# Second residual block: the gated unit's result and the new residual are transposed chunk by chunk, and the FFN norm's inverse root is applied after the up projection

## What is computed

```python
def second_block(x, ...):
    ...
    attn_out = attn @ w_attn_proj
    y = gelu(s5_scan(u, ...))
    ssm_out = (y @ w_glu_val) * sigmoid(y @ w_glu_gate)            # the gated unit
    mixed = sigmoid(g[:, :, 0]) * attn_out + sigmoid(g[:, :, 1]) * ssm_out
    h = h + mixed @ w_out                                          # the second residual
    m = h * rsqrt(mean(h * h, -1) + 1e-6) * norm_ffn               # the FFN norm
    h = h + (silu(m @ w_ffn_gate) * (m @ w_ffn_up)) @ w_ffn_down
    return h * rsqrt(mean(h * h, -1) + 1e-6) * norm_final
```

## Time and profile before

| | |
|---|---|
| median of 3 runs | 3183.25 us (3182.97 to 3200.63) |
| the profiled execution: its own time | 3179.22 us |
| the profiled execution: its span | 3177.4 us |
| TensorE busy (matmuls) | 3016.8 us, 95% of the span |
| VectorE, ScalarE, GpSimd busy | 57%, 40%, 10% |
| share of TensorE in the chain that ended last | 89% |
| mean granted TensorE clock | 0.97 of full speed |

### The profile page before, as it was taken

One profiled execution on the slowest core, in us unless ns is written; L12 is line 12 of the kernel. 1 busy time (PEld: TensorE's weight loads), 2 busy tenths in 40 slices (PEclk: granted clock), 3 DMA queues, 4 the chain that ended last, 5 costly groups with the idle time before them and its releaser, 6 DMA issues.

```text
span 3177.4 us, 43194 instructions
## 1 busy us (share of the span) xinstructions
PE 3016.8 (95%) x18045; PEld 2606.3 (82%) x18045; DVE 1804.6 (57%) x1704; ACT 1272.2 (40%) x1155; POOL 321.1 (10%) x460
## 2 busy tenths in 40 slices
PE   8899999996999999999698999989998999999998
PEld 3588777875999999888587888867877999999886
DVE  1376777787677776544545446754544444444444
ACT  0134544433444444344333333434433444444433
POOL 1000000001000000000105816620000000000000
PEclk9999999997999999999798999999998999999999
DMA  9777777893666655655345652226643555555564
GB/s 356 277 281 260 286 284 274 305 386 137 249 242 225 236 199 187 226 211 201 133 170 180 220 184 77 84 73 217 244 160 132 197 188 197 191 192 211 201 213 168
DMA packets 110499, 671.55 MB, mean 211 GB/s; under 512 B 23521, under 2 KB 25697, under 8 KB 33313
## 3 DMA queue, kind: packets, MB, share of 16 engines
q1 hardware_dynamic: 101584, 626.96, 54.7%
q0 software_dynamic: 8800, 42.97, 3.6%
HBM read 652.48 MB, written 17.40 MB: 211 GB/s over the span
## 4 chain that ended last, share of the span: by engine, by line
PE 89%; DVE 5%; DMA 3%; ACT 1%; issue 1%; SPq 0%; POOL 0%; DVEq 0%; POOLq 0%; ACTq 0%
PE acc L1800 27%; PE acc L1801 26%; PE acc L1802 26%; PE ms L1870 3%; PE tp L1845 2%; DVE w_lo L1130 1%; DMA w_raw<-ada_stream 1%; DMA w_raw<-w_stream 1%; DVE mod_sum L1205 1%; PE ms L2235 1%; PE acc L2264 0%; PE acc L2274 0%; DVE y L1171 0%; DMA ada<-ada_stream 0%; PE ms L2234 0%
## 5 line engine op out<-in xcount | busy, mean ns | idle before, releaser
L1130 DVE TENSOR_TENSOR w_lo<-w_raw,w_hi 128x2048 fp32r<-128x2048 f32 x484 | 1111.6, 2304 | 850.3 <-ACT w_hi L755 831.4
L755 ACT ACTIVATE w_hi<-w_raw 128x2048 fp32r<-128x2048 f32 x484 | 923.5, 1915 | 1071.3 <-DMA w_raw<-w_stream 1069.6
L1800 PE MATMUL acc<-h2T_hi,w_lo 128*128 128x256 f32 x2816 | 785.0, 279 | 3.5 <-DVE h2T_lo L1144 3.5
L1801 PE MATMUL acc<-h2T_lo,w_hi 128*128 128x256 f32 x2816 | 784.5, 279 | 0.0
L1802 PE MATMUL acc<-h2T_hi,w_hi 128*128 128x256 f32 x2816 | 784.4, 279 | 0.0
L1800 PEld LDWEIGHTS acc<-h2T_hi,w_lo 128*128 128x128 f32 x2816 | 530.3, 188 | 4.0 <-issue 4.0
L1801 PEld LDWEIGHTS acc<-h2T_lo,w_hi 128*128 128x128 f32 x2816 | 532.5, 189 | 0.0
L1802 PEld LDWEIGHTS acc<-h2T_hi,w_hi 128*128 128x128 f32 x2816 | 531.9, 189 | 0.0
L1800 PE MATMUL acc<-w_hi,hid_lo 128*128 128x512 f32 x704 | 275.1, 391 | 4.5 <-DVE w_lo L1130 4.5
L1801 PE MATMUL acc<-w_lo,hid_hi 128*128 128x512 f32 x704 | 274.8, 390 | 0.0
L1802 PE MATMUL acc<-w_hi,hid_hi 128*128 128x512 f32 x704 | 274.7, 390 | 0.0
(11 more groups left out here) (503 smaller groups left out, 3968.9 us busy)
## 6 DMA issues: line engine op xcount, KB each, us to landing
w_raw<-w_stream SPq DMA_DIRECT2D x484, 1024.0 KB, 4.8
ada<-ada_stream SPq DMA_DIRECT2D x64, 1024.0 KB, 6.9
w_raw<-ada_stream SPq DMA_DIRECT2D x32, 1024.0 KB, 4.8
g_dram<-gates_out SPq DMA_DIRECT2D x12, 512.0 KB, 7.0
gates_in<-g_dram POOLq DMA_DIRECT2D x12, 512.0 KB, 5.9
bias_rows<-b_in POOLq DMA_DIRECT2D x18, 256.0 KB, 6.2
x_res<-x POOLq DMA_DIRECT2D x2, 2048.0 KB, 13.6
g_dram<-gate_stage SPq DMA_DIRECT2D x8, 512.0 KB, 6.0
```

The costliest lines, as they stand in the source:

```text
L755: sc.activation(whi[:, s % 4], raw[:, s % 4], ACT.Copy).then_inc(hi_made, 1)
L1130: v.tensor_tensor(wlo[:, s % 4], raw[:, s % 4], whi[:, s % 4].bitcast(F32), ALU.subtract).then_inc(lo_made, 1)
L1800: mm(o, sl, mh, start=start, stop=False, skip_group_check=share)
L1801: mm(o, sh, ml, start=False, stop=False, skip_group_check=share)
```

## The change

- The transposes of `mix2` are issued in quarters (two rounds, one chunk's worth): quarters 0 to 2 between the gate and the value chunk of the next pair, quarter 3 after the second group of the first out2 chunk. The copies out of PSUM go with them on ScalarE and VectorE.
- The raw residual `x` is transposed in the same way: quarter n-1 after the second group of out2 chunk n, the last quarter after the second group of the first up chunk. The norm's gain `norm_ffn` is now a column (`gcol`, one value for each partition) and is applied in the copies out of PSUM: ScalarE copies with a scale, two instructions of 256 columns a round in place of one of 512, and VectorE takes `tp * gcol - hi`, also two a round. `m2` and the broadcast row `rowM` are gone.
- The squares of `x` are taken chunk by chunk, and GpSimd adds the first three chunk sums as they come.
- The inverse root is applied to the up projection's result. TensorE makes a row of it on all partitions (two matmuls with `rstd` broadcast and the identity, before the fourth group of the first up chunk), VectorE copies it to `rrow`. In each of the 22 up chunks VectorE multiplies the gate half by it before the Silu and the Silu's result by it before the product: two more VectorE instructions of 128x512.
- `x * norm_final` is formed chunk by chunk during the down projection; at the end `rstd` is applied to one token tile by VectorE and to the other by ScalarE.
- The loops of the gated unit and of out2, and the first two up chunks, are written out.

```diff
@@ -529,10 +530,12 @@
 
             def rsqrt_chunks(so_far):
 
+                q = ssq[:].rearrange("p (t c) -> p t c", c=4)
+                pool.wait_ge(sem("ysq"), so_far + 2)
+                chain(g.tensor_tensor(rstd[:, 0:2], q[:, :, 0], q[:, :, 1], ALU.add))
+                pool.wait_ge(sem("ysq"), so_far + 3)
+                chain(g.tensor_tensor(rstd[:, 0:2], rstd[:, 0:2], q[:, :, 2], ALU.add))
                 pool.wait_ge(sem("ysq"), so_far + 4)
-                q = ssq[:].rearrange("p (t c) -> p t c", c=4)
-                chain(g.tensor_tensor(rstd[:, 0:2], q[:, :, 0], q[:, :, 1], ALU.add))
-                chain(g.tensor_tensor(rstd[:, 0:2], rstd[:, 0:2], q[:, :, 2], ALU.add))
                 chain(g.tensor_tensor(rstd[:, 0:2], rstd[:, 0:2], q[:, :, 3], ALU.add))
                 chain(g.tensor_scalar(rstd[:, 0:2], rstd[:, 0:2], 1.0 / D, EPS, ALU.mult, ALU.add))
                 chain(g.tensor_tensor(rstd[:, 0:2], rstd[:, 0:2], mhalf[:, 0:2], ALU.pow))
@@ -727,6 +730,7 @@
...
             pool.wait_ge(sem("y_full"), KS)
             pool.wait_ge(sem("head_free"), 2 * KS)
             pool.wait_ge(sem("g_saved"), 16 * 8)
+            fetch("gcol", gcol, a["norm_ffn"])
             for n in range(8):
                 if n >= 2:
...
                     pool.wait_ge(pe_used, G_BEFORE_HEADS + G_HEADS + G_PROJ)
                     fetch("xre", x[:], a["x_dram"])
                 fetch(f"gate{n % 2}", gbuf[n % 2][:], a["g_dram"][n])
-            pool.wait_ge(sem("mixT"), 1)
-            fetch("rowM", rowM[:], bc(a["norm_ffn"]))
-            rsqrt_mean(D, [(P, 0, 2)])
+            rsqrt_chunks(8)
             pool.wait_ge(pe_used, N_GROUPS - G_DOWN)
             fetch("rowF", rowF[:], bc(a["norm_final"]))
-            rsqrt_chunks(8)
+            rsqrt_chunks(12)
 
         @block.scalar
         def _(act):
...
-            glu = Tally()
-            with engine_loop(act, 2, (m, 8), (glu, 2)) as i:
-                for j in range(2):
-                    for _ in range(2):
-                        split()
-                    act.wait_ge(pe_used, m.n - 2)
-                    sc.activation(gtmp[:, j], bank(0)[:], ACT.Sigmoid).then_inc(sem("glu_sig"), 1)
...
-            turns_hi(mxT[0], KD)
-            with engine_loop(act, 2, (m, 8)) as i:
-                for _ in range(8):
+
+            def hi_mix(n):
+                for k in range(2 * n, 2 * n + 2):
+                    turn_hi(mxT[0][:, 2 * k:2 * k + 2].rearrange("p a b -> p (a b)"))
+
+            def hi_x(n):
+                for k in range(2 * n, 2 * n + 2):
+                    act.wait_ge(tp_full, rounds.n + 1)
+                    for q in range(2):
+                        ins = sc.activation(h2T[0][:, 2 * k + q], tp[rounds.slot % 2][:, q * S:(q + 1) * S], ACT.Copy,
+                                            scale=gcol[:, 2 * k + q:2 * k + q + 1])
+                    ins.then_inc(tp_hi, 1)
+                    rounds.add()
+
+            for n in range(4):
+                split()
+                split()
+                act.wait_ge(pe_used, m.n - 2)
+                sc.activation(gtmp[:, n % 2], bank(0)[:], ACT.Sigmoid).then_inc(sem("glu_sig"), 1)
+                if n:
+                    hi_mix(n - 1)
+                split()
+                split()
+            split()
+            hi_mix(3)
+            act.wait_ge(sem("ld_gcol"), 16)
+            for n in range(4):
+                for _ in range(3):
                     split()
-            act.wait_ge(sem("x3"), 1)
-            squares(lambda k: x[:, k], lambda k: m2[:, k], P, (0, 1)).then_inc(sem("ssq"), 1)
-            turns_hi(h2T[0], KD)
+                chunk_squares(x, n, CH_OUT2 + n + 1)
+                if n < 3:
+                    split()
+                    hi_x(n)
             up2c = Tally()
 
-            def up2(c):
-                for _ in range(4):
+            def up2(c, first=False):
+                for q in range(4):
                     split()
-                act.wait_ge(pe_used, m.n - 2)
+                    if first and q == 0:
+                        hi_x(3)
+                act.wait_ge(sem("z_rms"), up2c.n + 1)
                 act.wait_ge(sem("hid_lo"), up2c.n + FC)
-                sc.activation(zc[:, 0:2], bank(up2c.slot)[:, 0].rearrange("p (f s) -> p f s", s=S),
-                              ACT.Silu).then_inc(sem("z_silu"), 1)
+                sc.activation(zc[:, 0:2], zc[:, 2:4], ACT.Silu).then_inc(sem("z_silu"), 1)
                 act.wait_ge(sem("z_mul"), up2c.n + FC + 1)
                 sc.activation(hid[0][:, bass.ds(c * 2, 2), :], zc[:, 0:2], ACT.Copy).then_inc(sem("hid_hi"), 1)
                 up2c.add()
 
-            with engine_loop(act, FC // 2, (m, 8), (up2c, 2)) as i:
+            up2(0, True)
+            up2(1)
+            with engine_loop(act, FC // 2 - 1, (m, 8), (up2c, 2)) as i:
                 for j in range(2):
-                    up2(i * 2 + j)
+                    up2(i * 2 + 2 + j)
...
                     split()
             chunk_squares(x, 3, CH_DOWN2 + 4)
+            act.wait_ge(sem("fin_row"), 1)
+            act.wait_ge(sem("rstd"), NORMS_X3 + 1)
+            sc.activation(fin[:, 1], fin[:, 1], ACT.Copy, scale=rstd[:, 1:2]).then_inc(sem("fin1"), 1)
...
+
+            def lo_mix(n):
+                for k in range(2 * n, 2 * n + 2):
+                    turn_lo(*(d[:, 2 * k:2 * k + 2].rearrange("p a b -> p (a b)") for d in (mxT[1], mxT[0])))
+
+            def lo_x(n):
+                for k in range(2 * n, 2 * n + 2):
+                    dve.wait_ge(tp_hi, los.n + 1)
+                    for q in range(2):
+                        ins = v.scalar_tensor_tensor(h2T[1][:, 2 * k + q], tp[rounds.slot % 2][:, q * S:(q + 1) * S],
+                                                     gcol[:, 2 * k + q:2 * k + q + 1], h2T[0][:, 2 * k + q].bitcast(F32),
+                                                     ALU.mult, ALU.subtract)
+                    ins.then_inc(tp_free[rounds.slot % 2], 1)
+                    los.add()
+                    rounds.add()
+
             for n in range(4):
                 finish(2)
                 dve.wait_ge(sem("glu_sig"), n + 1)
                 dve.sem_inc(acc_free, 1)
+                if n:
+                    lo_mix(n - 1)
                 finish(2)
                 j = n % 2
                 chain(tt(gtmp[:, j], bank(1)[:], gtmp[:, j], ALU.mult))
@@ -1727,53 +1769,63 @@
                 chain(tt(gtmp[:, j], gtmp[:, j], gbuf[j][:], ALU.mult))
                 dve.sem_inc(sem("g_used"), 1)
                 chain(tt(cols(mix2, n), cols(mix2, n), gtmp[:, j], ALU.add))
-            dve.sem_inc(sem("mix2"), 1)
-            turns_lo(mxT, KD)
-            turned()
-            dve.sem_inc(sem("mixT"), 1)
...
+                dve.sem_inc(sem("mix2"), 1)
+            split()
+            lo_mix(3)
             dve.wait_ge(sem("ld_xre"), 16)
...
-            dve.wait_ge(sem("ld_rowM"), 16)
+            dve.wait_ge(sem("ld_gcol"), 16)
+            for n in range(4):
+                b = finish(3)
+                tt(cols(x, n), b[:], cols(x, n), ALU.add).then_inc(acc_free, 1)
+                if n < 3:
+                    split()
+                    lo_x(n)
+            up2 = Tally()
+
+            def gated(c, first=False):
+                for q in range(4):
+                    split()
+                    if first and q == 0:
+                        lo_x(3)
+                    if first and q == 2:
+                        dve.wait_ge(sem("r_full"), 1)
+                        chain(v.tensor_copy(rrow, ms[0][:, 0:S]))
+                        norms.add()
+                b = finish(0)
+                r2 = rrow.unsqueeze(1).to_broadcast([P, 2, S])
+                tt(zc[:, 2:4], b[:, 0].rearrange("p (f s) -> p f s", s=S), r2, ALU.mult).then_inc(sem("z_rms"), 1)
+                dve.wait_ge(sem("z_silu"), up2.n + 1)
+                chain(tt(zc[:, 0:2], zc[:, 0:2], r2, ALU.mult))
+                chain(tt(zc[:, 0:2], b[:, 1].rearrange("p (f s) -> p f s", s=S), zc[:, 0:2], ALU.mult))
+                dve.sem_inc(acc_free, 1)
+                dve.sem_inc(sem("z_mul"), 1)
+                dve.wait_ge(sem("hid_hi"), up2.n + FC + 1)
+                hi, lo = (d[:, bass.ds(c * 2, 2), :] for d in hid)
+                v.tensor_tensor(lo, zc[:, 0:2], hi.bitcast(F32), ALU.subtract).then_inc(sem("hid_lo"), 1)
+                up2.add()
+
+            gated(0, True)
+            gated(1)
+            with engine_loop(dve, FC // 2 - 1, (m, 8), (chunks, 2), (up2, 2), (chain.t, 4)) as i:
+                for j in range(2):
+                    gated(i * 2 + 2 + j)
+            for n in range(4):
+                if n < 3:
+                    b = finish(12)
+                else:
+                    for _ in range(10):
+                        split()
+                    dve.wait_ge(pe_used, N_GROUPS)
+                    b = bank(chunks.slot)
+                    chunks.add()
```

(70 more changed lines are left out.)

53 lines of the change are left out of this document (5 added, 48 removed).

## The result

The kernel after took 3140.73 us (median of 4, 3139.02 to 3143.77) against 3184.45 for the kernel before in the same session: ratio 0.9856 [0.9815, 0.9896]. Measured again with more rounds it took 3143.51 against 3181.58: 0.9883 [0.9869, 0.9898]. The forecast, 3147.7 of 3183.25, is 0.9889. The profiled execution took 3143.77 us with a span of 3142.0; the forecast for it was 3143.7 and 3141.9. The median lies 0.7 us inside the range's lower edge, 3140; by the first ratio it would be 0.9856 x 3183.25 = 3137.4, under it. The forecast's ratio of 0.9889 lies inside both intervals.

What follows compares the result with a forecast made beforehand. TensorE bounds the kernel, with two gaps and a serial end. Middle 42.4 - 7.1 - 0.5 - 1.0 = 33.8 us, plus 1.7 at the end, gives 35.5: 3183.25 to 3147.7 us, forecast's own range 3145 to 3152, wider range 3140 to 3160.

Steps and rivals of the forecast that it cites:

- First gap: Between gated unit and out2: TensorE loses 15.4 us to mix2's finish and transposes, plus 1.7 us of half-clock matmuls.
- Quarters: Eight transposes among the matmuls of out2 and the first up chunk: 0.89 us each, eight cost 7.1 us.
- rstd matmuls: Two small matmuls spreading rstd over the partitions, in the first up chunk: cost 0.5 us, bounds 0.3 and 1.0.
- Stalls behind x quarters: TensorE waits for splits queued behind the residual quarters' copies: 0 to 0.6 us late, taken as 0.25 four times, 1.0 us.
- End: After the last matmul: fewer GpSimd additions and side-by-side scalings bring the end 1.7 us earlier, range 0.6 to 3.2.
- case of full sharing: Final stores: if they share bandwidth fully, 2 MB still take 6.6 us and the gain is 1.6 us; without sharing, 3.2.
- The up chunk's chain: Up projection: two new VectorE operations add 1.6 us per chunk, leaving 1.4 of 3.0 us margin; cost 0.
- Wait behind the x quarters: Rival: ScalarE's next split held longer, for instance by a 1.28 us table load in four places; 3152.8 us, chance 0.11.
- The clock: Rival: granted clock drops after each of eight quarters, 1.7 to 2.8 us each, 18 us back; 3165.7 us, chance 0.05.
- Does not do what it says: Rival: each second transpose round waits for its copies, so a quarter costs 2.8 us; 3162.9 us, chance 0.05.
- Slower by the chain: Rival: the up chunk's chain grows over 3.0 us and becomes the bound; at 5 us, 3191.7 us; chance 0.04.
- More than forecast: Rival: no stall, stores don't share bandwidth, smaller difference between profile and median; 3141 to 3145 us, chance 0.09.

Runs made afterwards that it cites:

- without cover: Kernel after, with each residual quarter issued as soon as its chunk ends, not two groups later; 3165.00 us, ratio 0.9953 to the kernel before.
- experiment 2: Kernel before plus only the mix2 quarters; residual, norm and end as before; 3170.26 us, ratio 0.9976 to the kernel before.
- 3: Kernel after without the mix2 quarters, whose transposes stand in one block before out2 again; 3152.53 us, ratio 0.9905 to the kernel before.
- experiment 6: Kernel after with every quarter's transposes issued twice; from the gated unit's first w_lo matmul to the end 919.7 us, 6.4 us more.
- experiment 8: Kernel after with one more weight group split ahead of each residual quarter's copies; 3143.85 us, ratio 0.986 to the kernel before.
- experiment 4: Kernel before plus only the new end (final gain moved into the down projection, last scalings side by side); 3177.21 us, ratio 0.9987.
- experiment 7: Kernel after with five more 128x512 VectorE operations in each up chunk; gated unit's first w_lo matmul to end 939.5 us, 26.2 more.
- experiment 12: Kernel after with one more pair of small fp32 matmuls in the second up chunk; gated unit's first w_lo matmul to end 931.3 us.

## Why the prediction was right or wrong

**The median: 7.0 us too high, and this is the step that failed.** The prediction took the profiled execution to the median by "the median of the runs is 4.0 us above the profiled one". For the kernel after it was 3.0 us below (3143.77 profiled, 3140.73 median): 4.0 + 3.0 = 7.0, the whole miss in the time. (The first measurement's gain, 43.7 us by the medians, exceeds the forecast by 1.2 more, because the kernel before took 3184.45 there and not 3183.25.) Nothing in the prediction gives a reason for the 4.0: they come from three runs of the kernel before, which lie up to 17.7 us apart. In its second measurement the same kernel after had its median 3.5 us above the profiled execution (3143.51 and 3139.97), so such an offset doesn't even keep its sign. It is scatter, and where two traces of one kernel can be compared, it lies ahead of the change: the two executions of the kernel after differ by 3.8 us, those of the kernel without cover by 6.4, and the stretches behind agree to 0.1. Part of it has a face: the 256-column matmuls of the first block's up projection go wide at different places in different executions, without cover at 427, 427, 435, 443 matmuls per 50 us from 800 us on in one and at 443, 443, 433, 427 in the next, same kernel. The second measurement's ratio (0.9883) is 0.0006 from the forecast's, and its median 4.2 us under the 3147.7. The offset should have been left out of the forecast and a like amount put on both sides of the range.

**The sum, 35.5 us: right** (35.4 between the profiled executions, 35.2 by the stretch, 35.6 by experiments 2 and 3). Middle 33.8 forecast, 33.8 by the last matmul. By terms:
- First gap: 17.1 less four quarters: 13.5 forecast; 13.7 (experiment 2), 13.3 (3).
- Quarters: 0.89 each forecast; 0.89 by the timeline, 0.87 for each added set in experiment 6.
- rstd matmuls: 0.5; 0.47. But they have a second effect, below.
- Stalls behind x quarters: four of 0.25, 1.0 us, forecast; three, idle for 0.9 us in the view of waits, and worth 0.6 by experiment 8, which takes them away. Right in cause; one fewer and 0.4 us smaller.
- Not in the sum: the up projection runs at the wide spacing up to the rstd matmuls, 0.6 us lost (below). This and the smaller stalls nearly cancel, which is luck.
- End: 1.7; 1.6 from the last matmul, in the kernel after and in experiment 4. The TENSOR_SCALAR estimated at 1.25 took 1.29, ScalarE's 2.00 (1.95); the second store is issued 0.8 us after the first and the end comes 6.7 us after the first is issued, as today: as the prediction's case of full sharing has it, the nearer of its two ends.

**The up chunk's chain: conclusion right, margin wrong.** The forecast had the chain 1.6 us longer, with 1.4 of 3.0 us left. The operations cost what was said, but the trace after shows no ACT_TABLE_LOAD in that stretch, where the loop before has two in two chunks. One load of 1.28 us fewer in each chunk nearly pays for the two operations. The kernels with the residual's part of the change (after, 3 and all made from after) have none; those without it (before, 2, 4) have them. That part writes out the first two up chunks, but it also changes what the Silu reads, and the two were not tried apart. For the writing out speaks the gated unit: its loop had four such loads (before, 4), and experiment 2, which writes it out and adds copies, has one. That the loop is then entered with the Silu's set already loaded, and the split's Copy is served by it, fits but was not tried. It was a gain that the prediction lacked; TensorE being the bound, it gave cover and no time.

**Rivals.** *Wait behind the x quarters*: no; the longest is 0.3 us and no table load stands there. *The clock*: no; 1.00 around eight quarters, and with them doubled. By the page cited in the prediction (the Trainium skill, TensorE: Matmul & The Clock Gate, Part 4) it might have fallen; for runs of 8 or 16 transposes between matmuls the trace does not agree. *Does not do what it says*: no; a quarter costs 0.89 and not 2.8. *Slower by the chain*: no, but experiment 7 shows the mechanism where it was said to be. *More than forecast*: it came closest to the time measured, and not for its reasons (stalls, stores) but for its last, the difference between profile and median.

**What the prediction lacked**: the risk of the wide spacing, some 18 us. The change removes the wait ahead of the up projection and adds a pair of small matmuls in it. Kernels that enter it from a wait (before, 2, 4, without cover) start close; those that enter straight from out2 (after, 3, 6, 8 and others) start wide, and the pair turns them close after 17.9 us (144 matmuls, 0.6 us lost). With the wait gone and no such pair the gain would be about half, an estimate from experiment 12, where the wide spacing from the second up chunk on leaves 948.5 - 931.3 = 17.2 us of the 35.2.

## What to carry to other kernels

A serial turn-around between two matmul stages (finish, transpose, split) can be cut by chunk and issued among the matmuls at its bare TensorE cost, if each piece has a cover of a chunk's half and the queue behind the copies is counted: here 42 us of gaps became 9. A change's size is read best within executions, from a point just ahead of it to the end; an offset between one profiled execution and the median is noise and belongs in the range, not in the forecast. Where TensorE is busy all the time at full clock, count its matmuls per window too: busy and clock don't show a spacing 4% wider.

## What the runs showed of the hardware

- The 256-column matmul stream has two steady spacings at granted clock 1.00, 0.1133 and 0.1175 to 0.1178 us (444 and 427 in 50 us), kept for hundreds of microseconds. It changes only where the stream is interrupted. In the second block a pair (or four) of small fp32 matmuls changes it each time and both ways (10 kernels with one such interruption, 2 with two), a quarter of eight or sixteen transposes never, and a wait of 0.3 to 0.8 us for a split sometimes (14 of 21 in experiment 7). In the first block it changes at some of the products of sums and added pairs, and at one small transpose in ten of 17 traces. What sets it stays open.
- Eight 128x128 fp32 transposes between matmuls cost 0.89 us and leave the granted clock at 1.00, as do sixteen (1.76 us).
- 20 loads of activation tables of 1.28 us between 2450 and 2890 us, one in each up chunk, are gone with the residual's part of the change, which writes two chunks out ahead of the loop. Whether the writing out does it was not tried apart.
